# Modulation loads two steps ahead, their groups spread over gate/up and the FFN output product, and ready work ahead of roundings, in a two-block transformer kernel

## What is computed

```python
def first_block(x, ...):                       # attention beside a recurrence, then FFN, then a gated add
    u = rms_norm(h, g_mix_pre) @ w_in
    q, k, v, xr, yg = jnp.split(u, ...)
    attn = neighborhood_attention(q, k, v, rpb)                 # 8 heads of 128
    rec = rglru_bidirectional(xr, ...) * jax.nn.gelu(yg)        # conv, gates, scans both ways
    mixed = jnp.concatenate([rms_norm(attn, g_attn_out), rms_norm(rec, g_rec_out)], axis=-1) @ w_out
    h = h + rms_norm(mixed, g_mix_post)
    fn = rms_norm(h, g_ffn_pre)
    ff = (jax.nn.silu(fn @ w_ffn_gate) * (fn @ w_ffn_up)) @ w_ffn_down    # inner width 5632
    h = h + rms_norm(ff, g_ffn_post)
    gate = jax.nn.sigmoid(rms_norm(h, g_ple_pre) @ w_ple_gate)
    return h + rms_norm(gate * (p @ w_ple_proj), g_ple_post)

def second_block(x, c, ...):
    mod = jax.nn.silu(c) @ w_ada + b_ada        # "modulation": 1 x 2048 by 2048 x 12288
    sh1, sc1, g1, sh2, sc2, g2 = split(mod, 6)
    h = layer_norm(x) * (1.0 + sc1) + sh1
    mix = token_mix(h, ...)                     # two attentions on latents, queries, keys
    x = layer_norm(DN_ALPHA * x + g1 * mix, ln1_g, ln1_b)
    h = layer_norm(x) * (1.0 + sc2) + sh2
    ffn = peer(h, w_pq, sub_key_1, sub_key_2, u_table, v_table)  # 16384 experts, top 16 of each of 8 heads
    return layer_norm(DN_ALPHA * x + g2 * ffn, ln2_g, ln2_b)
```

## Time and profile before

| | us |
|---|---|
| median of 3 runs | 3609.58 |
| lowest, highest | 3609.14, 3611.89 |
| profiled run | 3605.94 |
| its span (first to last instruction) | 3604.4 |
| mean granted clock of PE | 0.954 |
| PE busy | 3277.6 (91%) |
| DVE busy | 2069.3 (57%) |
| ACT busy | 1350.8 (37%) |
| POOL busy | 825.0 (23%) |

### The profile page before, as it was taken

How to read it: one execution, slowest core, us unless ns; L and a number is a source line. 1 busy time by engine, 2 the same in 40 slices (tenths; PEclk the granted TensorE clock), 3 DMA queues, 4 the chain that set the end, 5 groups by cost and what they waited for, 6 DMA issues and landing times.

```text
span 3604.4 us, 44367 instructions
## 1 busy us (share of the span) xinstructions
PE 3277.6 (91%) x16554; PEld 2650.4 (74%) x16554; DVE 2069.3 (57%) x2367; ACT 1350.8 (37%) x1371; POOL 825.0 (23%) x539
## 2 busy tenths in 40 slices
PE   7998788988999978798979699999999899999996
PEld 5987577777778843433557599888888788888885
DVE  5565767667665555543155688655555455555556
ACT  4555343333334420100143233455555344434342
POOL 2000000000000000000000378887888701000100
PEclk9999889999999989899989799999999999999998
DMA  6454656667655567577515246766666677666663
GB/s 222 165 175 164 222 193 245 227 221 251 227 197 189 197 245 297 186 285 278 219 60 172 86 159 194 208 213 216 214 210 212 175 257 245 240 241 239 244 242 136
DMA packets 195125, 753.97 MB, mean 209 GB/s; under 512 B 53936, under 2 KB 53968, under 8 KB 124384
## 3 DMA queue, kind: packets, MB, share of 16 engines
q1 hardware_dynamic: 129696, 664.84, 52.7%
q0 software_dynamic: 56128, 71.20, 7.0%
q10 hardware_dynamic: 9216, 16.78, 1.2%
HBM read 714.82 MB, written 37.93 MB: 209 GB/s over the span
## 4 chain that ended last, share of the span: by engine, by line
PE 60%; POOL 16%; DVE 10%; DMA 6%; issue 5%; ACT 2%; SPq 0%; DVEq 0%; POOLq 0%; ACTq 0%
POOL weight_dram L2559 15%; PE bank L599 12%; PE bank L600 12%; PE bank L601 12%; PE bank L453 10%; PE bank L605 7%; PE bank L606 3%; DMA misc<-in_w_ada 3%; DVE misc L1980 1%; DMA ring<-in_first 1%; DMA weight_dram<-misc 1%; PE bank L1075 1%; PE bank L437 1%; DMA big<-in_pproj 1%; DVE raw_lo L1793 1%
## 5 line engine op out<-in xcount | busy, mean ns | idle before, releaser
L2325 DVE TENSOR_TENSOR part_lo<-ring,part_hi 128x2048 fp32r<-128x2048 f32 x248 | 568.1, 2293 | 406.1 <-ACT part_hi L1684 386.5
L1684 ACT ACTIVATE part_hi<-ring 128x2048 fp32r<-128x2048 f32 x252 | 482.7, 1916 | 549.0 <-PE bank L601 293.2
L2559 POOL DMA_INDIRECT weight_dram<-misc x256 | 569.9, 2226 | 97.5 <-issue 91.1
L605 PE MATMUL bank<-h_both,part_hi 128*128 128x512 f32 x1664 | 578.5, 392 | 8.1 <-DVE part_lo L2325 8.1
L605 PE MATMUL bank<-h_both,ffn_hi 128*128 128x512 f32 x1408 | 514.7, 408 | 5.0 <-DVE big L2082 2.3
L606 PE MATMUL bank<-h_both,part_lo 128*128 128x256 f32 x1664 | 466.6, 280 | 0.0
L599 PE MATMUL bank<-part_hi,coef_hi 128*128 128x512 f32 x1024 | 399.5, 390 | 14.6 <-DVE part_lo L2325 13.6
L606 PE MATMUL bank<-h_both,raw_lo 128*128 128x256 f32 x1408 | 401.2, 285 | 0.0
L600 PE MATMUL bank<-part_lo,coef_hi 128*128 128x512 f32 x1024 | 399.3, 390 | 0.0
L601 PE MATMUL bank<-part_hi,coef_lo 128*128 128x512 f32 x1024 | 399.2, 390 | 0.0
L1980 DVE SCALAR_TENSOR_TENSOR misc<-misc,cact 128x512 f32<-128x512 f32 x360 | 270.4, 751 | 174.6 <-DMA misc<-in_w_ada 147.0
(11 more groups left out here) (363 smaller groups left out, 5545.8 us busy)
## 6 DMA issues: line engine op xcount, KB each, us to landing
ring<-in_u_table SPq DMA_DIRECT2D x128, 1024.0 KB, 5.0
ring<-in_v_table SPq DMA_DIRECT2D x128, 1024.0 KB, 4.9
misc<-in_w_ada SPq DMA_DIRECT2D x192, 512.0 KB, 5.8
ring<-in_gateup SPq DMA_DIRECT2D x88, 1024.0 KB, 5.0
ring<-in_first SPq DMA_DIRECT2D x56, 1024.0 KB, 5.0
ring<-in_stream SPq DMA_DIRECT2D x56, 1024.0 KB, 8.3
ring<-in_down SPq DMA_DIRECT2D x44, 1024.0 KB, 4.9
ring<-in_wo_pq SPq DMA_DIRECT2D x32, 1024.0 KB, 4.9
```

The source lines that it names most:

```text
L605: nc.tensor.matmul(out[:, 0:2 * S], hi, x_pair, start=start, stop=False)
L1684: a.activation(part_hi[j % PARTS], raw[j % RAW], ACT.Copy).then_inc(sem("hi_ready"), 1)
L2325: v.tensor_tensor(part_lo[j % PARTS], raw[j % RAW], part_hi[j % PARTS].bitcast(F32), ALU.subtract).then_inc(sem("lo_ready"), 1)
L2559: g_.indirect_dma_start(out=places, out_offset=bass.IndirectOffsetOnAxis(ap=gstage[:, t, k:k + 1], axis=0), in_=wstage[:, t, k:k + 1], in_ ...
```

## The change

The constants of the modulation groups change: one group before gate/up, eleven in all its rounds, seven in down (chunks 3 to 43, two or three accumulations a chunk by `down_ada`), four in pgate, one beside lat, none beside or after qk2. In gate/up a pair's load stands two steps before its use. In down their row sums go to banks that the running half doesn't use; the hidden parts move from misc, where the modulation ring lies, to nat and xT, two for each half. The hidden parts' rounding now goes before the chunk's, one step later. In gate/up the SiLU goes before the two roundings of its step, and the product before the accumulations. In the input projection, attention and wout, output copies, convolution, head steps and recurrence steps go before the rounding or remainder of the same step; wout uses six banks in turn. GpSimd's gate weights wait for the normalised x, the store of the projected p goes before the bias table, and the four selects wait for PE's chunks 12 to 15.

```diff
-ADA_EARLY = 2
-ADA_FFN = ADA_EARLY + KF // 4 - 1
+ADA_EARLY = 1
+ADA_DOWN = ADA_EARLY + KF // 4
+ADA_FFN = ADA_DOWN + 7
...
+DOWN_ADA = (ADA_FFN - ADA_DOWN) * KD
+def down_ada(m):
+    return range(max(m - 3, 0) * DOWN_ADA // (DOWN - 3), max(m - 2, 0) * DOWN_ADA // (DOWN - 3))
+def down_ada_loads(m):
+    def at(i):
+        return max(0, 3 + -(-(2 * i - 6) * (DOWN - 3) // DOWN_ADA))
+    return [i for i in range(2, DOWN_ADA // 2) if at(i) == m]
+def down_ada_ends(g):
+    return next(m for m in range(DOWN) if (g - ADA_DOWN + 1) * KD <= down_ada(m).stop)
...
# SyncE, gate/up and down
-                    if ada:
-                        ada_load(j, ADA_EARLY + it)
+                    ada_load((j + 2) % 8, ADA_EARLY + it + (j + 2) // 8)
...
-            gateup_round(KF // 4 - 1, RAW, ada=False)
+            gateup_round(KF // 4 - 1, RAW)
             for m in range(DOWN):
                 sp_.wait_ge(multiplied, gu_end + m - RAW + 1)
                 sp_.dma_start(ffn_raw[m % RAW], io["down"][m]).then_inc(raw_loaded[m % RAW], 16)
+                for i in down_ada_loads(m):
+                    ada_load(i % 8, ADA_DOWN + i // 8)
...
# TensorE
-                    if q == 0:
-                        wait_bank(pe, "wout", 2 * (i // 2) + 1)
+                    if q == 0 and i >= 6:
+                        pe.wait_ge(taken, out_no("wout", 2 * (i // 2) - 4))
...
+                if m == 1:
+                    pe.wait_ge(taken, out_no("down", 0))
+                    ada_sum(ADA_DOWN - 1)
+                for g in range(ADA_DOWN, ADA_FFN):
+                    if m == down_ada_ends(g) - 2:
+                        if g >= ADA_DOWN + 3:
+                            pe.wait_ge(taken, out_no("down", 4))
+                        ada_sum(g)
...
# ScalarE, attention and wout
+                    copy_out("yg", s_ - 1, ygT[:, s_ - 1, :], chunk=s_ - 1, width=S)
-                upper_in(n + 3)
                 if s_ == 1:
                     a.wait_ge(sem("rec_sum"), 1)
                 if s_:
                     at1.out(s_ - 1)
+                upper_in(n + 3)
...
# VectorE, gate/up round
                     summed(c, it)
-                    if not last:
-                        ada(2 * c, ADA_EARLY + it)
-                        ada(2 * c + 1, ADA_EARLY + it)
+                    if c % 2:
+                        hidden(c // 2, it)
+                    ada(2 * c, ADA_EARLY + it)
+                    ada(2 * c + 1, ADA_EARLY + it)
...
+                    if last and c >= 6:
+                        hidden_lo(c - 6)
                     if not (last and c >= 5):
                         ffn_lower(3 + c, it)
                     else:
                         down_lower(c - 5)
-                    if c % 2:
-                        hidden(c // 2, it)
...
# VectorE, down
             for m in range(3, DOWN):
+                if m % 2 == 0 and 2 <= m // 2 < 2 * HID_Q:
+                    hidden_lo(m // 2)
...
+                for i in down_ada(m):
+                    ada(i % KD, ADA_DOWN + i // KD)
+                    if i % KD == KD - 1:
+                        ada_end(ADA_DOWN + i // KD)
                 down_lower(m)
...
# GpSimd, start
+            g_.wait_ge(sem("x_normed"), 1 + T)
             g_.dma_start(rg_w.rearrange("p z g b c -> p (z g b c)"), io["rg"]).then_inc(sem("rg_in"), 16)
+            g_.wait_ge(sem("ple_copied"), 8)
+            g_.dma_start(ple_dram, pproj_out.rearrange("p t c -> p (t c)")).then_inc(sem("ple_stored"), 16)
...
+                    g_.wait_ge(multiplied, 13 + 2 * half + n)
```

More of the change, by code:

```diff
@@ L1456, in _ @@
                     at1.exps(s_ + 1)
[L1457 removed]
+                if s_ == 0:
+                    for t in range(T):
+                        copy_out("v", 2 + t, v1n[:, t, BAND:2 * BAND], chunk=7)
+                else:
                     copy_out("yg", s_ - 1, ygT[:, s_ - 1, :], chunk=s_ - 1, width=S)
[L1459 removed]
                 if s_ == 1:
```

236 lines of the change are left out of this document (109 added, 127 removed).

## The result

The changed kernel took **3435.52 us** (median of 4 runs, 3432.43 to 3437.03) against 3610.73 us for the kernel before on the same chip: a ratio of 0.9513, 95% interval 0.9496 to 0.9529. Measured once more in a later set it took 3435.36 us, ratio 0.9528 (0.9515 to 0.9541).

The account below looks back on a forecast made before the run. It took TensorE's idle time, chiefly gate/up waits for DVE's marker, as the bound. Savings 74 - 18 + 43.5 + 14 + 27 + 6 = 146.5 us gave span 3457.9, plus 1.5 and 3.7: 3463 us, range 3440 to 3512.

Parts of the forecast that it names:

- Gate/up: Gate/up stage: loads two steps ahead remove ten pauses, saving 74 us (51 waits, rest half-clocked work), bounds 51 to 80.
- rival 5: Gate/up: the clock gives back half of all half-clocked time, saving 87 us in place of 74, total 3450 us; chance 0.05.
- Down: FFN output product: loses 18 us: +8 row sums, +3 accumulator waits, +7 passage from gate/up; bounds 9 to 35.
- rival 2: FFN output product becomes bound by DVE or DMA, leaving no room for waits, total 3508 us; chance 0.12.
- Latent and query products: Stretch up to the transposes after the query products: seven modulation groups leave, saving 43.5 us, bounds 38 to 46.
- Front: Stages before the norm: start saves 14 us, attention 6, output projection 27.
- The early traffic: Start: delaying gate weights and bias table lands x and projection weights 2 to 4 us earlier, closing a 4.08 us gap.
- The selects: Start: moving GpSimd's four mask selects off DVE's softplus steps saves 8.8 us, plus 3 of slow clock.
- Norm behind it: Norm after the output projection: a DVE and ACT chain the change doesn't shorten, so 0 saved.
- 1: Gate/up keeps a pause of 2 us a round with 1.3 of slow clock, total 3499 us; chance 0.13.
- 3: Start and projection: early reordering fails because weights, not order, hold them; 37 us lost, total 3500 us; chance 0.08.
- 4: Down: the ring of four modulation pairs falls into lockstep, +179 us in place of +18, total 3624 us; chance 0.02.

## Why the prediction missed, point by point

**Gate/up: mechanism right, size too small.** 74 forecast, 85.7 measured, and the load distance alone gives 84.8. The pauses (51) and the slow clock behind them (10 x 2.25: sum 0.85, steps 1.4) are as worked out. The step that failed is the chunk length: 5.7 us from k-steps of 0.353 to 0.359. I took a stretch between two pauses for undisturbed work. It was not: it held a restart's longer step (0.3533 against 0.3467, worth (0.3516 - 0.3474) x 1408 = 6 us by the stages' means) and short stops for the hidden product (4 us in all, half of it in one stop). With 2 us at the start of the stage that is 12, the difference. In the changed kernel a chunk takes 16 x 0.3467 = 5.55 us, not 5.69. The second reading of the clock, rival 5, gave 87 and so came nearer, but for a reason that the timelines don't bear out: of the 69 us at the lower level in this stage's clock records 14 lie in PE's stops themselves, and what follows a pause in slow work is 2.25 us a round, not 3.6. The rule for the penalty that I set beside it (the Trainium skill, "TensorE: Matmul & The Clock Gate", section Terms) is an upper bound here: it gives 34 to 36 us, and the rounds show 22.5.

**Down: right.** The passage was worked out to 5.4 us and is 5.48, each station within 0.2 us of the estimate, with 1.5 us of slow clock behind it for the 1.3 in the sum. Eight sums cost 9 us and not 8. The 3 us of waits at the accumulator were 0.2. My DVE load was too high (the accumulations take 0.749 and not 0.84 us), so rival 2's reason, too little room on DVE, was weak in size. But its concern was real: with 31 us more work the stage loses 18, in waits at the row sums. One slip bore on nothing: 72 loads of 1 MB (1.05 million bytes) in 230 us are 328 GB/s; the 316 goes with 239 us, and 304 were measured.

**Latent and query products: right**, 44.9 against 43.5; PE doesn't stop, and nothing came late behind.

**Front: 54.2 against 47.** By stage, start, projection and attention gave 19.7 of 20 forecast, and the miss is the output projection's, 34.6 against 27. I had counted it from its second chunk on, where at most 31 us were to be had, and left four of them for one wait. No wait came (31.6), and the first chunk, which I hadn't counted though PE's gap of 2.79 us stood at its end, gave 3.0 more.

What each edit gives is less clear. The early traffic is worth 6.7 (forecast 2 to 4), and its cause I had only half: not 2 MB of gate weights but the small pieces, perhaps with them. The selects are worth 11.4 (forecast 8.8 + 3), but that the numbers agree is luck: they cost it in the convolution, where I had the softplus. The order in projection and attention costs 19.4 when undone, against 6 forecast for attention, but a part of that is the 6.51 us gap in the third chunk with its slow clock, which comes back when either the selects or the order are undone. In the output projection banks cost 6 and order 9. Since two edits can guard the same gap, the prices don't add up to the gain, and how the 54 splits by edit, the moved modulation group included, stays open. I had looked for what each edit removes, and not for which gaps two of them share.

**Norm behind it:** 0 forecast, 1.5 gained, not followed up.

**The step from span to median.** I added 5.2 us, what the kernel before had between them. The changed kernel had 0.1 (and -0.6 in the repeat). Of the 5.2, about 1.5 stand between the time of a run and its span in every run; the other 3.7 were chance, since the profiled execution of before was faster than any of the runs in its set, and they should have stood in the range, not in the sum. The changed kernel's profiled run was by chance 1.5 slower than its median. That is 5 of the 27.5 us. Gate/up is 12, the front 7, the norm, down and the products 4.

**The range** ended at 3440 although all high ends together gave 3433. I reasoned that not all fall alike. But two high ends were themselves too low, gate/up's 80 (85.7 measured) and the output projection's 31 (34.6): the one because work read in a kernel with gaps contains the gaps' after-effects, the other because a chunk was left out.

**Rivals.** Nothing showed of 1 (no pause left), of 3 (the front gave more than forecast) or of 4: the ring kept up at 304 GB/s in down, and the landing of down's chunks grew from a median of 4.9 to 7.2 us, far from my estimate of 15 at which it would lock.

## What to carry to other kernels

Price undisturbed work from the shortest steps that the trace has anywhere, not from the mean between two stops; the difference to the mean is a part of what removing the stops gives back. When loads of another stream are spread over a stage, look at the queue's order where stages meet: five loads ahead of the next stage's first cost 6 to 8 us and moving them is free. An accumulator that two engines pass back and forth can make them wait for each other though neither is full; a second one together with a later sum took the waits away. When such a stop goes, look at what released it before: one that looked like the accumulator's was a bank's.

## What was not expected of the hardware

- A k-step of TensorE at full granted clock has two lengths, 0.3467 and 0.3533 us. The longer one follows stops, even of 0.9 us with no change of the clock (6 of 10), hardly ever a row sum without a stop (3 of 150), and usually stays to the next break of the stream; why is open.
- One of GpSimd's mask selects (2.5 us) holds up one DVE instruction beside it for most of its length: 0.41 becomes 2.55 us, two in a row 5.27 instead of 1.00, and a remainder of 2.29 becomes 4.42.
- In down DMA brought 304 GB/s over the whole stage, with all engines but GpSimd working on the same memory, and PE kept its step.
